# The last stage of a three-block kernel: which chain units finish before the first output tile, and where each load, root and subtraction stands in the queues

## What is computed

```python
def hybrid_layer_3(x, ...):                      # x: (1, 2048, 1024)
    h = x @ w_in + b_in
    q_a, k_a, v_a, g_a, q_h, z_fwd, z_bwd, i_h, g_h = split(h)        # nine parts of 512
    o_a = neighbourhood_attention(q_a, k_a, v_a, rpb) * silu(g_a)
    o_fwd = hgrn2_chunk_scan(qh, k_f, ih, logf_f)                     # a recurrence forwards
    o_bwd = flip(hgrn2_chunk_scan(flip(qh), flip(k_b), flip(ih), flip(logf_b)))   # and backwards
    o_h = o_fwd + o_bwd                                               # 4 heads of 128
    o_h = o_h * rsqrt(mean(o_h ** 2, axis=-1) + 1e-6) * hg_norm_gain * silu(g_h)
    y = concat(o_a, o_h) @ w_out + b_out
    r = layer_norm(2 ** 0.25 * x + y)
    return r
```

## Time and profile before

| what | value |
|---|---|
| device time, median of 3 executions | 4405.23 us |
| lowest and highest of them | 4396.6 and 4409.22 us |
| the profiled execution's own time | 4401.29 us |
| its span, first to last instruction | 4399.5 us |
| granted TensorE clock, mean over the span | 0.981 of full speed |
| TensorE busy (matmul) | 4193.7 us, 95% of the span |
| VectorE (DVE) busy | 2709.1 us, 62% |
| ScalarE (ACT) busy | 1755.9 us, 40% |
| GpSimd (POOL) busy | 664.9 us, 15% |
| busy share of TensorE by fortieths of the span | `6999999999999999999989989999999999999699` |

### The profile page before, as it was taken

How to read it: one execution, slowest core, us unless ns; L and a number is a source line. 1 busy time by engine, 2 the same in 40 slices (tenths; PEclk the granted TensorE clock), 3 DMA queues, 4 the chain that set the end, 5 groups by cost and what they waited for, 6 DMA issues and landing times.

```text
span 4399.5 us, 61981 instructions
## 1 busy us (share of the span) xinstructions
PE 4193.7 (95%) x24248; PEld 3425.2 (78%) x24266; DVE 2709.1 (62%) x4274; ACT 1755.9 (40%) x3389; POOL 664.9 (15%) x308
## 2 busy tenths in 40 slices
PE   6999999999999999999989989999999999999699
PEld 5888888889888877788767758877787787777577
DVE  6788888872566642134467767656556556466587
ACT  5111111111466641122366646545445446445540
POOL 3111111110333321111011111332000000000021
PEclk9999999999999999999999999999999999999799
DMA  5111111122544431112389892478666566555653
GB/s 186 44 53 53 53 53 53 53 67 88 186 133 127 128 132 39 67 49 79 115 279 293 284 309 106 157 258 284 224 218 201 165 208 201 180 193 190 211 178 134
DMA packets 514987, 663.42 MB, mean 151 GB/s; under 512 B 60476, under 2 KB 407424, under 8 KB 491274
## 3 DMA queue, kind: packets, MB, share of 16 engines
q1 hardware_dynamic: 465402, 573.45, 40.3%
q10 hardware_dynamic: 49296, 86.00, 5.2%
HBM read 441.98 MB, written 217.38 MB: 150 GB/s over the span
## 4 chain that ended last, share of the span: by engine, by line
PE 79%; DVE 7%; DMA 6%; ACT 4%; issue 2%; SPq 1%; POOL 1%; ACTq 0%; another core or an unknown queue 0%; DVEq 0%; POOLq 0%
PE ps L229 11%; PE ps L230 11%; PE ps L231 11%; PE ps L3841 3%; PE ps L3842 3%; PE ps L3843 3%; PE ps L255 3%; PE ps L254 3%; PE ps L256 3%; DMA w_split_tiles<-w 2%; PE ps L3958 2%; PE ps L242 1%; PE ps L243 1%; PE ps L244 1%; PE ps L2242 1%
## 5 line engine op out<-in xcount | busy, mean ns | idle before, releaser
L229 PE MATMUL ps<-hh,wsplit 128*128 128x512 f32 x2048 | 820.6, 401 | 4.0 <-DVE hl L953 3.0
L230 PE MATMUL ps<-hl,wsplit 128*128 128x512 f32 x2048 | 809.3, 395 | 0.0
L231 PE MATMUL ps<-hh,wsplit 128*128 128x512 f32 x2048 | 808.3, 395 | 0.0
L982 DVE SCALAR_TENSOR_TENSOR conv_acc<-conv_in,pcol,conv_acc 128x1024 f32<-128x1024 f32 x480 | 687.4, 1432 | 14.8
L230 PEld LDWEIGHTS ps<-hl,wsplit 128*128 128x128 f32 x2048 | 390.5, 191 | 91.9 <-issue 4.3
L229 PEld LDWEIGHTS ps<-hh,wsplit 128*128 128x128 f32 x2048 | 386.9, 189 | 96.0 <-issue 7.3
L231 PEld LDWEIGHTS ps<-hh,wsplit 128*128 128x128 f32 x2048 | 389.1, 190 | 89.2
L221 POOL TENSOR_TENSOR wsplit<-wraw,wsplit 128x1024 fp32r<-128x1024 f32 x72 | 204.1, 2845 | 1326.6 <-ACT wsplit L216 1326.6
L3841 PE MATMUL ps<-h_hi,w 128*128 128x512 f32 x896 | 378.3, 422 | 8.9 <-DVE h_lo L3070 4.4
L3842 PE MATMUL ps<-h_lo,w 128*128 128x512 f32 x896 | 358.3, 400 | 0.0
L3843 PE MATMUL ps<-h_hi,w 128*128 128x512 f32 x896 | 356.9, 398 | 0.0
(11 more groups left out here) (421 smaller groups left out, 8704.7 us busy)
## 6 DMA issues: line engine op xcount, KB each, us to landing
w<-w_split_tiles SPq DMA_DIRECT2D x108, 1024.0 KB, 5.3
wraw<-in_w_in SPq DMA_DIRECT2D x72, 512.0 KB, 4.0
w_split_tiles<-w SPq DMA_DIRECT2D x36, 1024.0 KB, 7.2
sh<-hy_ak ACTq DMA_DIRECT2D x48, 512.0 KB, 4.0
g_tiles<-b_ost SPq DMA_DIRECT2D x80, 256.0 KB, 5.5
w_raw<-in_w_in SPq DMA_DIRECT2D x36, 512.0 KB, 4.7
wo_raw<-in_w_out SPq DMA_DIRECT2D x32, 512.0 KB, 5.8
sh<-hy_ad ACTq DMA_DIRECT2D x32, 512.0 KB, 9.6
```

The costliest lines, as they stand in the source:

```text
L229: e.matmul(p[:, :], wh, c.HH[tb][:, k, :], start=k == 0, stop=False)
L230: e.matmul(p[:, :], wh, c.HL[tb][:, k, :], start=False, stop=False)
L231: t = e.matmul(p[:, :], wl, c.HH[tb][:, k, :], start=False, stop=k == 7)
L982: e.scalar_tensor_tensor(v, a[:, h * 1024 + j:(h + 1) * 1024 + j], c.convw(j, ch), v, ALU.mult, ALU.add) \
```

## The change

- Units 1 and 4 exchange their chain buffers (`chain_buffer`), and the loads of the first units are spread over the steps: unit 0, unit 2, unit 1, unit 3, unit 4, each with waits of its own in place of one wait for all stores ahead of unit 1.
- Chain units from 5 on stand three steps later. `o0` is one step earlier (c0 + 8). So units 0 to 4 come before the first output tile, and unit 5 and later behind it; before, units 0 to 8 came before it.
- The roots of units 0 to 3 are split: `fin_log` (the logarithms of units 0 to 2 one step before that of unit 3) and `fin_exp` (the exponentials of the 128 columns of the first tile for all four units, then of the other 384 columns). `fin2` of units 0 to 3 follows: first the 128 columns of all four, then the 384 of each. Unit 4's chain stands between.
- `fin_root` of a later pair comes one step earlier relative to its units, and `fin2` too.
- Output weights: blocks 4 to 7 are loaded from step c0 - 2 on; the high part of blocks 0 to 3 is taken in step c0 - 3, of blocks 4 to 7 in step c0. The low part (`wo_low`) of blocks 0 to 3 is taken on POOL in pieces of 256 columns, that of blocks 4 to 7 on DVE, 128x1024 at a time, after the first tile's `y_split`.
- The first tile's product (`first_out`) does both halves together, in three parts: all high x high, then all low x high, then all high x low.
- `o_const` comes in step c0 + 1, which is behind unit 4's loads on SP. In `rank`, `y_ld` goes from 7 to 21: behind the stores of `fin2` in the same step.

```diff
     for k in range(8):
-        after((143, 144, 141, 142)[k] if k < 4 else c0 + 1, "wo", k)
-    for k in range(0, 8, 4):
-        after(c0 if k < 4 else c0 + 7, "wo_split", k)
+        after((143, 144, 141, 142)[k] if k < 4 else c0 - 2, "wo", k)
+    o0 = c0 + 8
+    after(c0 - 3, "wo_split", 0)
+    after(c0, "wo_split", 4)
+    after(c0, "wo_low", 0)
+    after(o0 - 1, "wo_low", 4)
     for n in range(16):
-        s = c0 + n
-        after(c0 - 5 if n < 1 else c0 if n < 5 else c0 + 2 if n < 10 else c0 + 9 if n < 12 else c0 + 11 if n < 14 else c0 + 13, "ch_ld", n)
+        s = c0 + n + (3 if n > 4 else 0)
+        after(c0 + ((-5, -1, -3, 0, 0, 3, 4, 8, 9, 10)[n] if n < 10 else 11 if n < 12 else 13 if n < 14 else 14), "ch_ld", n)
         after(s + 1, "chain", n)
         after(s + 2, "ch_o", n)
         after(s + 3, "sq", n)
         after(s + 3, "fin", n)
-        if n == 3:
-            after(s + 3, "fin_root", 0, 1, 2, 3)
+        if n == 2:
+            after(s + 3, "fin_log", 0, 1, 2)
+        elif n == 3:
+            after(s + 3, "fin_log", 3)
+            after(s + 3, "fin_exp", 0, 1, 2, 3)
             after(s + 3, "fin2", 0, 1, 2, 3)
         elif n % 2 and n > 3:
-            after(s + 4, "fin_root", n - 1, n)
-            after(s + 5, "fin2", n - 1, n)
-    o0 = c0 + 9
-    after(c0 + 5, "o_const")
+            after(s + 3, "fin_root", n - 1, n)
+            after(s + 4, "fin2", n - 1, n)
+    after(c0 + 1, "o_const")
     after(o0 - 1, "o_scale")
...
-            "ld": 0, "w_st": 0.2, "val": 1, "turn": 2, "qk": 3, "bias": 4, "out": 0.3, "state": 0.4, "prod": 3.5, "y_ld": 7, "ch_o": 8, "sq": 8.2, "o_root": 8.4, "chain": 9, "o_sum": 9.5, "o": 10, "o_end": 11, "y_split": 12, "o_norm": 13, "fin": 19, "o_st": 24, "x_ld": 25, "ch_ld": 26, "values": 27}
+            "ld": 0, "w_st": 0.2, "val": 1, "turn": 2, "qk": 3, "bias": 4, "out": 0.3, "state": 0.4, "prod": 3.5, "y_ld": 21, "wo_low": 22, "ch_o": 8, "sq": 8.2, "fin_log": 19.5, "fin_exp": 19.6, "fin2": 19.7, "o_root": 8.4, "chain": 9, "o_sum": 9.5, "o": 10, "o_end": 11, "y_split": 12, "o_norm": 13, "fin": 19, "o_st": 24, "x_ld": 25, "ch_ld": 26, "values": 27}
...
-            if n == 0:
-                for u in (first_of(3, 0) + 2, first_of(3, 0) + 3):
+                for u in (first_of(3, hd) + 2, first_of(3, hd) + 3):
                     e.wait_ge(*L.qe_st[u % 4][u])
                     e.wait_ge(*L.kv_st[u % 2][u])
-                stored((3, "rg", 0))
+                stored((3, "rg", hd))
+            if n == 2:
+                e.wait_ge(*L.r_dve[63, "qe"])
+                e.wait_ge(*L.r_act[63, "dec"])
+                for q in L.ost_st:
+                    e.wait_ge(*q.end())
             elif n == 1:
+                for q in L.y_st:
+                    e.wait_ge(*q.end())
+            elif n == 3:
                 e.wait_ge(*L.r_pe[63, "out", 1])
-                for q in L.qe_st + L.kv_st + L.ost_st:
-                    e.wait_ge(*q.end())
             elif n == 4:
-                for q in L.y_st:
+                for q in L.qe_st + L.kv_st:
                     e.wait_ge(*q.end())
...
+def w3_out_low(e, L, q, o, m):
+    lo, raw, hi = L.WO[:, q, 1024 + o:1024 + o + m], L.WOraw[:, q, 1024 + o:1024 + o + m], L.WO[:, q, o:o + m]
+    return e.tensor_tensor(lo, raw, hi, ALU.subtract)
 def chain_buffer(n):
-    return n if n < 10 else 11 - n if n < 12 else n - 8
+    return {1: 4, 4: 1, 10: 0, 11: 4, 12: 1}.get(n, n if n < 10 else n - 8)
...
+    def first_out():
+        p, y = [take_bank(e, c, ("out", 3, 0, h), L.pb) for h in range(2)], L.Y2[y_buffer(0)]
+        e.wait_ge(*L.o_act["hi", 0])
+        for part in range(3):
+            if part == 1:
+                e.wait_ge(*L.o_dve["lo", 0])
+            for k in range(8):
+                if part == 2:
+                    e.wait_ge(*(c.wo_lo_pool[3, k, 3] if k < 4 else c.wo_lo_dve[3, k]))
+                for h in range(2):
+                    w = L.WO[:, k, 1024 * (part == 2) + h * 512:1024 * (part == 2) + (h + 1) * 512]
+                    o = 1024 * (part == 1) + k * 128
+                    t = e.matmul(p[h][:, :], y[:, o:o + 128], w, start=part == 0 and k == 0, stop=part == 2 and k == 7)
+                    if part == 2 and k == 7:
+                        t.then_inc(*L.o_pe.up((0, h)))
```

More of the change, by code:

```diff
@@ L3308, in b3_sp @@
             if i == 6:
-                e.wait_ge(*L.ch_pe[15])
-                e.wait_ge(*L.ch_dve[15, 0])
+                n = next(q for q in range(10, 16) if chain_buffer(q) == 0)
+                e.wait_ge(*L.ch_pe[n])
+                e.wait_ge(*L.ch_dve[n, 0])
+                e.wait_ge(*L.ry_st[n % 4][n])
             elif i >= 2:
@@ L3814, in b3_pool @@
             w3_low(e, c, s[1])
-        elif k == "wo_split":
-            for q in range(s[1], s[1] + 4):
+        elif k == "wo_low" and s[1] == 0:
+            for q in range(4):
                 e.wait_ge(*L.wo_hi[q])
-                e.tensor_tensor(L.WO[:, q, 1024:2048], L.WOraw[:, q, 1024:2048], L.WO[:, q, 0:1024], ALU.subtract).then_inc(*c.wo_lo_pool.up((3, q)))
+                for m in range(4):
+                    w3_out_low(e, L, q, 256 * m, 256).then_inc(*c.wo_lo_pool.up((3, q, m)))
         elif k == "x_ld":
@@ L3995, in b3_pe @@
             i, h = s[1:]
+            if i == 0:
+                if h == 0:
+                    first_out()
+                continue
             def before(k):
```

34 lines of the change are left out of this document (26 added, 8 removed).

## The result

| | before | changed |
|---|---|---|
| median of 20 runs each, in turn on one chip | 4404.1 us | 4416.4 us |
| lowest to highest | 4396.6 to 4411.5 | 4405.6 to 4423.6 |
| profiled execution, its span | 4401.3, 4399.5 us | 4412.5, 4410.7 us |
| granted TensorE clock over the span | 0.981 | 0.982 |

The ratio is 1.0026, with an interval of 1.0019 to 1.0032: the change costs 12 us. That is still within the 0.3% called no change, and 4416 lies inside the range (4385 to 4418), but the interval leaves 1 out. The forecast, 4404 and no difference, missed a small, real slowdown.

A forecast was written before the change was run, and what follows sets the result against it. The prediction saw a 57 us hole in block 3's tail, then a stretch bounded by TensorE. Its terms, -27.3 + 6.9 - 6.0 + 25, summed to -1.4 us, giving 4404 us, range 4385 to 4418.

The forecast's parts named there:

- Rival 1: Output tiles: y loads arrive in time despite standing behind stores, waits only 9 us, 4388 us; chance 0.2.
- The start: Block 3's tail: first product at about 4166, 25.5 us earlier; first tile ends at 4178.9, 27.3 us earlier.
- the bound on unit 4's and unit 3's loads: Ahead of the first tile: unit 4's products taken to end at 4154, with bounds of 4149 and 4160.
- the 4170: Sign of being wrong: the first output product starting after 4170, instead of at 4162 to 4170.
- Rival 3: Tail's start: unit 4's loads queue behind 2 MB of weights and land at 4160 or later, +6, 4410 us; chance 0.1.
- Work pushed behind: Behind the first tile: five units and three sums on TensorE that the hole used to hide, +6.9 us.
- waits that go: Behind the first tile: TensorE's old idle time and half-clock products from a DVE and SP loop disappear, -6.0 us.
- Waits that come: Output tiles: y loads behind stores on SP make TensorE wait, together +25 us, bounds 9 and 38.
- The walk through the tiles: Waits followed half by half: 3.1, 2.4, 5.8, 3.6, 0.9, 3.8 and 5.0 us, from tile 2 to tile 8.
- Spacings forecast as 18.0: Tiles 3 to 8: y splits about 18 us apart, where TensorE needs 14.7; from tile 9 on 11.2.
- Rival 2: Output tiles: POOL's bias adds collide with DVE's work, 1.9 us for six tiles, +11 us, 4415 us; chance 0.15.
- The sum: Whole kernel: -27.3 + 6.9 - 6.0 + 25 = -1.4 us, forecast as no change at 4404 us.

The follow-up runs named there:

- e2_yfirst: The change, with the y loads of tiles 3, 5, 7 and 8 issued on SP ahead of the next pair's waiting store: 4402.8 us.
- e3_wolate: The change, with the last four weight loads put behind the units' loads again and their high parts made later on ACT: 4419.4 us.
- e12_unit1late: The change, with unit 1's four loads (1 MB) issued behind the last store of the recurrence instead of ahead of it: 4412.6 us.
- e9_mix_root4: e2_yfirst with chain steps of units 6 to 15 one half tile earlier, but pairs' roots and finish left where e2_yfirst has them: 4403.3 us.
- e6_yfirst_nobias: e2_yfirst with GpSimd's bias addition cut to one of 1024 columns, so the output lacks the others' bias: 4396.4 us.
- e10_yfirst_fin2: e2_yfirst with each pair's four finishing operations on VectorE moved ahead of their half tile's state updates, residual sum and normalisation: 4427.1 us.
- e11_early2: The change, with units from 7 a whole tile earlier, unit 6 half, some unit loads earlier, y loads from tile 3 ahead of stores: 4413.2 us.

## Why the prediction was right or wrong

**Right in its shape.** The first product early, a price behind it, its place (y loads behind the stores of a pair, tiles 3 to 8) and its size of some 25 us were as written; that the two would balance was not. e2_yfirst shows that place to be the cause of the slowdown: undoing it for tiles 3, 5, 7 and 8 alone gives 15 us back. Rival 1, "the y loads come in time", didn't come true in the change, and in e2_yfirst only in half, as tiles 4 and 6 still wait, and there the time was 4402.8, not 4388.

**The start, predicted -27.3, measured -21.1.** The step that failed is the bound on unit 4's and unit 3's loads. Unit 3's "loads wait until the last kv and o stores have landed, which ACT's four weight conversions push back by some 2 us" was written, and priced at those 2 us. The store's issue did move by that much (16.8 us behind the mark before, 18.6 now), but the wait behind it was 8.1: its own landing had grown from 2.4 us to 8.6, for which no term stood. Unit 4's products ended 42.2 us behind the mark, where 35.8 (4154) had been taken, and the first product came 5.6 us late; that the landing is what delays them is read from the timelines, no run took it away. At 4175.27, or 4171.5 without the scatter of the mark, it is past the 4170 that the prediction named as a sign of being wrong. The tile itself took 13.6 us instead of 12.9; its first products, up to about 4180, ran at a granted clock of 0.50 to 0.59. Rival 3, "the start does not move that far", is thus what happened, and in the main by another road than the weights that it named (e3_wolate, e12_unit1late).

**Work pushed behind and waits that go, +6.9 and -6.0.** Nothing speaks against them; the runs don't measure them apart from what follows.

**Waits that come, predicted +25, measured 28.5** (215.4 - (186.0 - 6.0) - 6.9). The mechanism was right and the size too small, and what it is made of was wrong: idle time is 18.0 us, not "some 25", and the other 10 are products at half clock behind the waits. The walk through the tiles counted no such price, though I had read one in the rows of before (1.9 us behind a wait of 2.9). Spacings forecast as 18.0, with more ahead of tile 4, came out as 18.7, 20.7, 16.8, 19.6, 16.1, 16.1.

**Rival 2, "the bias adds collide"**, was a part of the truth rather than a rival: priced at +11 us for six tiles, measured at some 8 us in the change; the kernel before had 2.6, which can't be told from nothing. By the Trainium skill, SBUF — State Buffer, section "Who interferes with whom", a VectorE instruction with two inputs in SBUF and a GpSimd one that reads SBUF exclude each other for a whole instruction. The trace agrees, with the 2.49 us of an update of 0.35. Not every addition hits: of the first seven in the change four fall on updates, two on the low parts of the weights, where nothing waits, and one on the scaling of the residual (2.01 us instead of 1.27).

**The sum.** -27.3 + 6.9 - 6.0 + 25 was -1.4; the same terms as measured are -21.1 + 6.9 - 6.0 + 28.5 = +8.3. With the scatter of 3.7 and -1.0 at the end they give 11.0 of the 11.2 us between the profiled spans. The medians differ by 12.3 us, so some 5 us of the measured slowdown are not in these terms. Two terms, both of waits, were too kind, by 6.2 and 3.5 us, both in the same direction. A forecast whose large terms cancel to -1.4 should not be centred on what is left of them: each unpriced thing here (landing of stores under load, clock behind a wait, collisions) added to the time.

**A better version?** e2_yfirst and e9_mix_root4 beat the change by 0.3%, and stand at 0.9992 and 0.9995 to the kernel before, which is no measured difference. Only e6_yfirst_nobias is below it (0.9975), and it leaves the bias out. That says where some 7 us may be won next, by moving the bias addition out of the time that POOL and VectorE share; the waits of tiles 4 and 6 that e2_yfirst still has are the other place. No run here wins either of them with the bias left in.

## What to carry to other kernels

When a change moves one stream by a half period against another, go through every queue that both share and ask in which order their operations now stand: here one place on SP (load behind store) cost 15 us, and one on ACT and VectorE (a pair's roots ahead of the high part, and its finish with them) 25 us, at equal work. Price a TensorE wait as its idle time plus the slow products behind it, and the landing of a store by what is in the queues at that moment, not by its landing when they were empty. And an instruction that waits costs what is queued behind it, so moving it forward in its queue (e10_yfirst_fin2, e11_early2) is only a gain if what it waits for is already there.

## What the hardware showed that I had not expected

- A store of 256 KB that landed 2.4 us after its issue with no load just ahead of it took 7.8 to 10.0 us with two units' loads and four weight loads ahead (ten executions), 8.6 with the weights and one unit's loads (e12_unit1late), 6.9 with two units' loads alone (e3_wolate).
- A single VectorE update of 0.35 us took 2.49 us when it began together with a GpSimd addition of 2.36: the wait is for the other's whole instruction, and one hit on a short update stops TensorE for 2.0 us.
- The same code ahead of the tail brought the tail's start anywhere from 4117.65 to 4128.76 in 14 profiled executions, about as much as the whole effect studied here. Two profiles can only be compared from a mark behind which they differ, and even from there the same code scattered by 3.7 us up to the first product.
